# Mix's first two tiles turned and split, and the first one multiplied, at the end of attention's block

## The reference

```python
h = rmsnorm(x, g_attn)
qa, ka, va, qb, kb, vb = split(h @ w_in)
oa = window_sink_attention(qa, ka, va, sink_a, rel_bias)      # band of 128 around each query
ob = axial_qknorm_attention(qb, kb, vb, gq_b, gk_b)           # dense
mixed = concatenate([rmsnorm(oa, g_out_a), rmsnorm(ob, g_out_b)])
x = x + mixed @ w_out                                         # "Mix"
x = x + expert_choice_moe(rmsnorm(x, g_ffn), w_router, w_gate, w_up, w_down)
x = x + sigmoid(rmsnorm(x, g_ple) @ w_ple_gate) * (p @ w_ple_proj)
y = rmsnorm(x, g_final)
```

## Time and profile before

| | |
|---|---|
| median of 3 runs | 1466.58 us (1465.59 to 1468.96) |
| profiled execution | 1468.08 us, its span 1466.3 us |
| mean granted TensorE clock | 0.985 of full |
| PE busy | 96% of the span |
| DVE, ACT, POOL busy | 63%, 49%, 13% |

### The profile page before, as it was taken

How to read it: one execution, slowest core, us unless ns; L and a number is a source line. 1 busy time by engine, 2 the same in 40 slices (tenths; PEclk the granted TensorE clock), 3 DMA queues, 4 the chain that set the end, 5 groups by cost and what they waited for, 6 DMA issues and landing times. The chain is left out here.

```text
span 1466.3 us, 21296 instructions
## 1 busy us (share of the span) xinstructions
PE 1403.2 (96%) x7154; PEld 986.6 (67%) x7154; DVE 924.2 (63%) x1449; ACT 715.2 (49%) x1142; POOL 190.6 (13%) x257
## 2 busy tenths in 40 slices
PE   7999998999999989799999899999999999979997
PEld 5888886655565555588888565666666665648885
DVE  5644446777778887236888667667666676633343
ACT  5444436776667877222214545444445444523332
POOL 1211110000000000011002111112211121021221
PEclk9999999999999999899999999999999999999998
DMA  9544456152212231534336778877887778752331
GB/s 352 172 146 156 150 182 232 68 215 97 78 61 97 71 132 65 189 132 155 121 122 221 302 295 276 275 254 250 273 258 254 270 255 267 257 146 91 142 127 72
DMA packets 83031, 266.79 MB, mean 182 GB/s; under 512 B 8688, under 2 KB 36976, under 8 KB 67488
## 3 DMA queue, kind: packets, MB, share of 16 engines
q1 hardware_dynamic: 74752, 238.80, 45.1%
q0 software_dynamic: 7168, 25.17, 7.5%
q10 hardware_dynamic: 1056, 2.11, 0.4%
HBM read 201.55 MB, written 66.60 MB: 183 GB/s over the span
## 5 line engine op out<-in xcount | busy, mean ns | idle before, releaser
L2201 DVE TENSOR_TENSOR edge_w_lo<-ring,edge_w_hi 128x2048 fp32r<-128x2048 f32 x95 | 218.1, 2296 | 134.0 <-ACT edge_w_hi L2138 134.0
L2138 ACT ACTIVATE edge_w_hi<-ring 128x2048 fp32r<-128x2048 f32 x94 | 180.2, 1918 | 184.6 <-PE moe_p_g L2346 104.9
L1841 PE MATMUL mix_p_big<-kept_out_w,mix_m_hi 128*128 128x512 f32 x384 | 126.1, 410 | 5.6 <-DVE mix_x L1665 3.0
L1214 DVE TENSOR_REDUCE attend_ntop<-attend_p_s 128x1 f32<-128x1024 f32 (+1 forms) x96 | 100.2, 1044 | 47.9 <-PE attend_p_s L1005 47.1
L582 PE MATMUL proj_p_out<-proj_w_hi,proj_h_hi 128*128 128x512 f32 x288 | 116.8, 406 | 9.3 <-DVE proj_w_lo L494 8.1
L1019 PEld LDWEIGHTS attend_p_t<-kept_ident_r,attend_probs_r 128*128 128x128 f32 x896 | 96.0, 140 | 36.1 <-ACT attend_probs L1151 11.7
L2354 PE MATMUL moe_p_gu<-ring,moe_xT_r 128*64 128x512 f32 x512 | 116.9, 598 | 0.0
L1019 PE MATMUL attend_p_t<-kept_ident_r,attend_probs_r 128*128 128x128 f32 x896 | 106.8, 243 | 9.3 <-ACT attend_probs L1151 5.6
L582 PE MATMUL proj_p_out<-proj_w_hi,proj_h_lo 128*128 128x512 f32 x288 | 113.0, 392 | 0.0
L582 PE MATMUL proj_p_out<-proj_w_lo,proj_h_hi 128*128 128x512 f32 x288 | 112.8, 392 | 0.0
L1151 ACT ACTIVATE attend_probs<-attend_p_s,attend_ntop 128x1024 f32<-128x1024 f32 (+1 forms) x96 | 93.4, 974 | 20.7 <-DVE attend_ntop L1214 19.6
(11 more groups left out here) (283 smaller groups left out, 2964.2 us busy)
## 6 DMA issues: line engine op xcount, KB each, us to landing
ring<-in_w_gate SPq DMA_DIRECT2D x32, 1024.0 KB, 5.8
ring<-in_w_up SPq DMA_DIRECT2D x32, 1024.0 KB, 7.0
ring<-in_w_down SPq DMA_DIRECT2D x32, 1024.0 KB, 5.8
qT_d<-proj_qT SPq DMA_DIRECT2D x11, 1024.0 KB, 3.9
proj_xT<-in_xT SPq DMA_DIRECT2D x12, 512.0 KB, 4.0
proj_w_raw<-in_w_in SPq DMA_DIRECT2D x8, 768.0 KB, 6.6
proj_x<-in_x SPq DMA_DIRECT2D x12, 512.0 KB, 5.3
ahead_q<-qT_d SPq DMA_DIRECT2D x6, 1024.0 KB, 5.3
```

The lines of the kernel that those rows point to most:

```text
L1214: dve.tensor_reduce(ntop[:, s, head:head + 1], p_s[:, head % 2, 0:part.T], AX.X, ALU.max, negate=True).then_inc(ntop_done, 1)
L1841: mm = pe.matmul(p_out[:, cols], m[:, s, k, :], ww[:, k, cols], start=(k == 0 and n == 0), stop=(k == KC - 1 and n == 2))
L2138: act.activation(w_hi[:, at % SPLIT], raw[:, at % RAW], ACT.Copy).then_inc(hi_made, 1)
L2201: dve.tensor_tensor(w_lo[:, at % SPLIT], raw[:, at % RAW], w_hi[:, at % SPLIT].bitcast(F32), ALU.subtract).then_inc(lo_made, 1)
```

## The change

In attention's block, behind the last tile's loop, three things are added. PE turns Mix tile 0 (`turn_next(0)`) before the last `values_b` and tile 1 before the last `turn_o_b`, into the scores' PSUM tile `p_s`; ACT and DVE split them (`high_next`, `low_next`) into `m_hi`, `m_lo`, which now lie in the part of `pT_b` that prompt tiles don't use. Behind `turn_o_b` PE multiplies tile 0 with `w_out` (`product_next`), into `p_o` and `p_ot`. SP loads x of tile 1 and, once a tile is turned, tiles 2 and 3 into its place. Mix's block then leaves these steps out: PE starts with the product of tile 1, DVE adds x to the two halves in `p_o` and `p_ot`, the counters are filled by `sem_inc`, and the product of tile 1 has no x1 to wait for. In step 2 `turn_h(0)` goes behind the second half product. `norm(0)` takes over the wait for `g_all` and `w_r`. The prompt weights are split behind step 3 (before step 4) instead of at the start.

```diff
@@ attend: SP, behind the loop
             following.load_first(sp)
-            for i in (N - 2, N - 1):
-                store(i, A)
-                store(i, B)
+            store(N - 2, A)
+            store(N - 2, B)
+            sp.wait_ge(z_made, N)
+            following.load_x(sp, slice(P, 2 * P), 1)
+            for t, g in enumerate((A, B)):
+                sp.wait_ge(next_turned, t + 1)
+                following.load_m(sp, slice((t + 2) * P, (t + 3) * P), t)
+                store(N - 1, g)
@@ attend: PE
+            def turn_next(t):
+                pe.wait_ge(following.m_landed[t], 16)
+                if t == 0:
+                    pe.wait_ge(exp_done, N * 16 - 1)
+                else:
+                    pe.wait_ge(next_lo, t)
+                for k in range(KC):
+                    mm = pe.transpose(next_mT[:, k, :].bitcast(F32R), following.m_r[:, t, k * P:(k + 1) * P], ident_r[:])
+                mm.then_inc(next_turned, 1)
+            def product_next():
+                w_hi, w_lo = w.hi, w.lo
+                pe.wait_ge(next_lo, 1)
+                pe.wait_ge(w.lo_made, KC)
+                for c, p_out in enumerate((p_o, p_ot)):
+                    pe.wait_ge(*((oT_out[B], N) if c == 0 else (o_made[B], N)))
+                    cols = slice(c * BANK, (c + 1) * BANK)
+                    for k in range(KC):
+                        for n, (m, ww) in enumerate(((following.m_hi, w_hi), (following.m_hi, w_lo), (following.m_lo, w_hi))):
+                            pe.matmul(p_out[:].rearrange("p a b -> p (a b)"), m[:, 0, k, :], ww[:, k, cols],
+                                      start=(k == 0 and n == 0), stop=(k == KC - 1 and n == 2))
             for head in (14, 15):
                 turn(prompt, N - 1, head, False, False)
+            turn_next(0)
             for j in VALUES_B_STEPS:
                 values_b(prompt, N - 1, j)
+            turn_next(1)
             turn_o_b(N - 1)
+            product_next()
@@ attend: ACT
+            high_next(0)
             square(N - 1, A)
             out_of_psum(N - 1, B, False)
+            high_next(1)
             square(N - 1, B)
@@ attend: DVE
             rows(N - 1, A)
             share_b(N - 1, 1)
+            low_next(0)
             mean_of(N - 1, A)
             normalise(N - 1, A)
             rows(N - 1, B)
+            low_next(1)
             mean_of(N - 1, B)
             normalise(N - 1, B)
@@ mix_and_route: SP
-                if later(t, 2):
+                if later(t, 4):
                     sp.wait_ge(mT_made, t - 1)
                     sp.sem_inc(sp_turn, 1)
-                inputs.load_m(sp, at, s)
+                    inputs.load_m(sp, at, s)
...
-            inputs.load_x(sp, rows(1), 1)
@@ mix_and_route: ACT
-                if inside(t):
+                if inside(t) and later(t, 2):
                     high(t, s)
...
-            high(0, 0)
+            for t in range(1, 4):
+                step(t, t % 2)
             for k in range(PC):
                 w_p.high(act, k)
-            for t in range(1, 4):
-                step(t, t % 2)
@@ mix_and_route: DVE
+                if isinstance(t, int) and t == 0:
+                    for c, product in enumerate(inputs.first_out):
+                        cols = slice(c * BANK, (c + 1) * BANK)
+                        added = dve.tensor_tensor(x1[:, s, cols], product[:].rearrange("p a b -> p (a b)"), x_sb[:, s, cols],
+                                                  ALU.add)
+                    added.then_inc(x1_made, 1)
...
             def norm(t, s):
+                if isinstance(t, int) and t == 0:
+                    dve.wait_ge(g_landed, 32)
...
-                if inside(t):
+                if inside(t) and t >= 2:
                     low(t, s)
...
+            for done, count in ((mT_made, 2), (m_hi_made, 2), (m_lo_made, 2), (mm_done, 2)):
+                dve.sem_inc(done, count)
             dve.wait_ge(blank, 3)
-            low(0, 0)
-            for k in range(PC):
-                w_p.low(dve, k)
-            dve.wait_ge(g_landed, 32)
             for t in range(1, N):
+                if t == 4:
+                    for k in range(PC):
+                        w_p.low(dve, k)
@@ mix_and_route: PE
-                    if later(t, 1):
+                    if later(t, 2):
                         pe.wait_ge(x1_made, t)
...
-                if inside(t - 1):
+                if inside(t - 1) and later(t, 2):
                     product(t - 1, 1 - s, 0)
-                if inside(t):
+                if inside(t) and later(t, 2):
                     turn_m(t, s)
                 if inside(t - 3):
                     turn_aff(t - 3)
-                if inside(t - 2):
+
+                first = isinstance(t, int) and t == 2
+                if inside(t - 2) and not first:
                     turn_h(t - 2, s)
-                if inside(t - 1):
+                if inside(t - 1) and later(t, 2):
                     product(t - 1, 1 - s, 1)
+                if first:
+                    turn_h(0, 0)
                 if inside(t - 2):
                     logits(t - 2)
...
-            turn_m(0, 0)
             run(pe, step, N)
```

More of the change, by code:

```diff
@@ L810, in attend @@
         mixed = ahead.mixed
+        following.begin_early(nc.sbuf_base - 4 * KC // 2 * D)
         p_s = a.ps("p_s", [P, 2, 2 * BANK])
@@ L814, in attend @@
         p_ot = a.ps("p_ot", [P, GROUP, P])
+        following.first_out = p_o, p_ot
         halves = sem("halves")
         late_turned, late_copied = sem("late_turned"), sems("late_copied", 2)
+        next_turned, next_hi, next_lo = sem("next_turned"), sem("next_hi"), sem("next_lo")
         nsink_made = sem("nsink_made")
@@ L856, in attend @@
         SPLIT_ORDER = (5, 6, 7, 0, 1, 2, 3, 4)
+        next_mT = p_s[:, 0, :].rearrange("p (k q) -> p k q", k=KC)
         def split_next(part, i, j):
@@ L1185, in _, with high_next @@
             run(act, tile)
+            def high_next(t):
+                act.wait_ge(next_turned, t + 1)
+                if t == 0:
+                    act.wait_ge(w.lo_made, KC)
+                act.activation(following.m_hi[:, t, :, :], next_mT, ACT.Copy).then_inc(next_hi, 1)
             for head in (14, 15):
                 copy_turned(act, 0, prompt, N - 1, head, False, False, copy)
+            high_next(0)
             square(N - 1, A)
             out_of_psum(N - 1, B, False)
+            high_next(1)
             square(N - 1, B)
@@ L1283, in _, with low_next @@
                 copy_turned(dve, 1, prompt, N - 1, head, False, False, copy)
+            def low_next(t):
+                dve.wait_ge(next_hi, t + 1)
+                dve.tensor_tensor(following.m_lo[:, t, :, :], next_mT, following.m_hi[:, t, :, :].bitcast(F32),
+                                  ALU.subtract).then_inc(next_lo, 1)
             rows(N - 1, A)
             share_b(N - 1, 1)
+            low_next(0)
             mean_of(N - 1, A)
@@ L1322, in __init__, with begin_early @@
         self.m_landed, self.x_landed = held.sems("mix_m_landed", 2), held.sems("mix_x_landed", 2)
+    def begin_early(self, at):
+        self.m_hi, self.m_lo = (self.nc.alloc_sbuf_tensor_at(f"mix_{n}", [P, 2, KC, P], F32R, offset=at + 8 * D * i)
+                                for i, n in enumerate(("m_hi", "m_lo")))
+        self.parts_at, self.parts_end = at, at + 16 * D
     def load_m(self, sp, at, s):
@@ L1403, in mix_and_route @@
         early, late = start.early, start.late
-        m_hi, m_lo = (early.sb(n, [P, 2, KC, P], F32R) for n in ("m_hi", "m_lo"))
-        x1, (h_sb, h_r) = early.sb("x1", [P, 2, D]), early.sb_both("h", [P, 2, D])
+        m_hi, m_lo = inputs.m_hi, inputs.m_lo
+        x1 = early.sb("x1", [P, 2, D])
+        assert early.low <= inputs.parts_at
+        early.low = inputs.parts_end
+        h_sb, h_r = early.sb_both("h", [P, 2, D])
         w_p_raw, g_all = early.sb("w_p_raw", [P, PC, D]), early.sb("g_all", [P, D])
@@ L1664, in add_x @@
                     dve.wait_ge(x1_stored[s], before(t, s))
-                dve.tensor_tensor(x1[:, s, :], p_out[:], x_sb[:, s, :], ALU.add).then_inc(x1_made, 1)
+                if isinstance(t, int) and t == 0:
[4 more added lines that the diff above has]
+                    added.then_inc(x1_made, 1)
+                else:
+                    dve.tensor_tensor(x1[:, s, :], p_out[:], x_sb[:, s, :], ALU.add).then_inc(x1_made, 1)
             def norm(t, s):
+                if isinstance(t, int) and t == 0:
+                    dve.wait_ge(g_landed, 32)
                 dve.wait_ge(rooted, t + 1)
```

## The result

| | before | changed |
|---|---|---|
| median, same chip, 5 runs each | 1466.58 us (1464.27 to 1470.00) | 1455.67 us (1454.38 to 1458.39) |
| ratio | | 0.9931 (95%: 0.9917 to 0.9945) |
| profiled execution, its span | 1468.08, 1466.3 | 1455.67, 1453.6 |
| mean granted TensorE clock | 0.985 | 0.985 |

The kernel is faster by 0.69% (0.55 to 0.83%), that is 10.1 us (8.1 to 12.2). This goes by the ratio, which has an interval; the table's two medians are 10.9 us apart. Forecast were 8.0 us and 1458.6, range 1454.6 to 1462.4.

The account below looks back on a forecast made before the run. PE was taken as the bound, busy 1403.2 of 1466.3 us. The third tile's product starts 9.6 us earlier, less 1.6 for one clock fall: 8.0 us net, 1466.6 to 1458.6 us, range 1454.6 to 1462.4.

Parts of the forecast that it names:

- The sum of the stretch: From attention's last turn to the third tile's product: 37.02 us before, that product 9.6 us earlier after the change.
- wait for `hT`: Before tile 0's logits in Mix, PE waits for ACT's copy of `hT`, no longer covered by a half product: 1.1 us.
- PE as the last to arrive at a block change: Between attention and Mix, PE restarts 0.45 us after arriving last; bounded above by 3.95 us.
- rival 2: Part given back: PE's restart takes 3 us more, or two more clock falls; gain 5.0 or 4.8 us; chance 0.12.
- h of tile 0 in time: Mix's start: h ready at 610.8, PE wants it at 614.6, so 3.8 us of cover.
- rival 3: Slower: `norm(0)` waits for late `g_all` and `w_r`; gain gone if they land at 621.3; chance 0.02.
- Edits at no cost: Moved loads, prompt weights' split before step 4 and `sem_inc` counters cost nothing; the split, if uncovered, 2.5 us once.
- The clock in step 2: Mix's step 2: 3.5 us without dense products brings one fall of the clock, costing 1.6 us.
- Rival 1: No clock fall in step 2, or one less elsewhere: gain 9.6 us, 1457.0; chance 0.27.
- The clock in values_b: Attention's last values_b, at clock 0.50 until 588: eight more turns before it bring nothing there.
- Rival 4: The added turns keep the clock up in values_b: up to 1.65 us less, 1457.0; chance 0.04.
- Behind that the step is the old one: After the third tile's product starts, the step is unchanged and bound by PE alone, so the stretch's gain is the kernel's.

Follow-up runs that it names:

- Turning and splitting only: The changed kernel with the product of tile 0 left in Mix's block, turning and splitting of both tiles staying in attention: 1464.09 us, ratio 0.9987.
- eight turns: The kernel before with only the eight transposes of Mix's tile 0 added ahead of the last values_b, result unused: median 1465.89 us, ratio 0.9997.

## Why the prediction was right, point by point

- **The sum of the stretch.** Forecast 9.6 us from the last turn to the third tile's product; measured 37.02 - 27.31 = 9.7, or 9.9 from the start of that turn in both. Each term: turns and splits 0 (nothing on PE's path waits for them), two halves of the product 5.69 each (5.58, from 589.98 to 595.56), block change 0.45 (0.54), wait for `hT` 1.1 (1.11), product of tile 1 to the turn 5.69 (607.38 - 601.76 = 5.62).
- **PE as the last to arrive at a block change.** The trace of before had no row for it, and I took the row with the same role over the one nearby (0.88) and the upper bound (3.95). All six profiles with the product in front show 0.54. The row names DVE's queue at L1863 as the releaser, which fills the counters, so PE's own restart may be shorter. The 3 us of rival 2 didn't come.
- **h of tile 0 in time.** Forecast 3.8 us of cover; h done at 608.03, wanted at 613.58, cover 5.5. It is more because `w_r` landed 4.3 us after its issue, at 606.1, and not 5.9 us after, at 609.4. Landing 6.5 us later did cost, as rival 3 had it.
- **Edits at no cost.** True of the new place of the weights' split: DVE's idle of 4.20 us shrank to 1.85. What I didn't say is what the old place would cost: 6.7 us, two thirds of the gain. I asked what the new place costs and not what the old one would do once tile 0's `add_x` is the first thing DVE is wanted for.
- **The clock in step 2** is the step that failed. I read from two falls behind shorter pauses that the longer one would bring a fall, most of the time, and took 1.6 us off. It came in one profile of three (and not in the one of "Turning and splitting only", which has the same stretch) and then cost 3.2 us. Rival 1 (no fall, 1457.0) was the likelier case, and 10.1 us measured are nearer to 9.6 than to 8.0. That the measured gain lies above both is no merit of the sum: the half products below gave 1.6 us that it didn't have.
- **The clock in values_b.** Rival 4 (the turns keep it up) had 0.04. Its rows came, but the time didn't: the fall was in the first profile of before and in only one of four later ones. So the guess that this profile's 1.5 us over the median are about one fall fits the later profiles: the other three profiles of before, without a fall in values_b, have spans of 1462.2 to 1463.6 against 1466.3 and 1465.3. The Trainium skill (TensorE: Matmul & The Clock Gate, Part 4: PE-mode transpose) says that transposes don't count as PE activity in the way that matmuls do. Nine of nine profiles at full clock with eight more transposes, beside three of five without, don't confirm it, and with 1 chance in 9 don't refute it either.
- **What no step had:** Mix's half products are faster from tile 2 on. See the last section; over 20 half products of tiles 2 to 11 that is 1.6 us. "Behind that the step is the old one" was thus not quite true, nor were the later waits for x1 the same: 0.30, 0.34 and 0.92 us before, 0.17, 0.48, 0.35, 0.40 and 0.55 us in the changed kernel's first profile, 0.4 us more.
- **The books.** Against a typical execution of before: 44.1 - 34.1 = 10.0 us in the stretch, 1.6 in the half products, less about one fall more in Mix's later steps (before: two in each of five profiles, changed kernel: three, two and three, apart from step 2; 1.6 us each; rival 2's two more falls came in part) and less the occasional fall in step 2 (3.2 us in one of three). That is 10.0 + 1.6 - 1.1 - 1.1 = 9.4, or 9.0 with the waits, within the measured 8.1 to 12.2. The rows up to the first expert's product bear it out. Counted from the last head turns it starts after 230.5 to 232.1 us in the kernel before (mean of five profiles 231.1) and after 220.8, 222.5 and 220.8 us in the changed kernel (mean 221.3), 9.8 less, of which 0.7 is the fall in values_b that two of the five had. Behind Mix the executions of either kernel differ by 3 us among themselves.

## What to carry to other kernels

At a block change look for dense work of the next block whose inputs are ready before the change, and put it in front, where a serial tail of small operations leaves PE idle: it covers the tail, keeps the clock up and hides the next block's start, while moving only the small preparations (turn, split) brought little of that here (1.9 of 10.1 us, at most 3.4). Then check what the other engines' queues hold first behind the change, since work that used to hide there may now delay the first result that is wanted. And take several profiles before a fall of the clock enters a sum: the same kernel shows it in one execution and not in the next. A row that ends at the start of the next instruction also holds the wait between them: take the wait out before putting a longer time down to the clock.

## What the runs showed that I had not expected

**Half products of Mix take 5.59 us in place of 5.67**, from tile 2 on. In all seven profiles of kernels with the old layout (five of before, two with eight turns) those without a fall take 5.65 to 5.71 us; in all seven with the new layout 5.56 to 5.63. Tile 1's second half is an exception: in two of the seven (the second profile of the changed kernel, and "Turning and splitting only") it takes 5.66 at full clock in the new layout too. A half product of the changed kernel without a fall, from its start to the turn behind it (before: 613.32 to 619.01 in the earlier trace rows):

```profile
631.55 0.71 PE L1911 MATMUL mix_p_big<-kept_out_w,mix_m_hi 128*128 128x512 f32 x2
...
637.15 0.79 PE L1900 MATMUL mix_p_big<-kept_ident_r,mix_m_r 128*128 128x128 f32 x8
```

The instructions of the later steps are the same in both. What differs is where `m_hi`, `m_lo`, `h` and their neighbours lie in SBUF, and when the steps run. That the placement does it is a guess; no run moved the buffers alone.

**A fall can last twice as long.** In step 2 of the changed kernel's second profile the clock was at 0.50 from about 615.9 to 622.6, for 3.2 us lost, where a fall in Mix's later steps costs 1.6 (7.25 against 5.69 in the earlier trace rows). In the kernel before, the fall in the hole itself lasted longer in two of five profiles, which cost 0.2 us of distance.
